# Layer 1's prompt attention: the two softmax maps summed on VectorE before PE transposes them

## The chip, the cores and the metric

The kernel runs on one NeuronCore of a Trainium2 chip. The metric is the device time of one execution in microseconds (us), from start to end of the program. The engines are called as the profile calls them: PE is TensorE (PEld its weight loads), DVE is VectorE, ACT is ScalarE, POOL is GpSimd, SP is the sync engine, which here only issues DMAs. PE's clock has two levels, 1.2 and 2.4 GHz; the profile gives the granted clock as a share of the higher one.

## What is computed

One inference step of a two-layer decoder: a prompt of 512 tokens and 8 sample sequences of one token each, with 2048 cached positions. Layer 0 is gated linear attention, layer 1 is differential attention over a shared key and value; each layer ends in a mixture of 16 experts. The part that matters here is layer 1's attention of the prompt, for 8 heads and 4 query blocks of 128 rows:

```
q1, q2 = q[..., :64], q[..., 64:]            # both maps have 64 columns of q and k
p1 = softmax(q1 @ k1.T + bias, axis=-1)      # bias: causal, ALiBi
p2 = softmax(q2 @ k2.T + bias, axis=-1)
o  = (p1 - lam * p2) @ v
```

In the same stage the sample sequences attend to their paged cache: for each sequence 16 pages of 128 keys and 128 values.

## The kernel before, in words

`stage_decoder` does both attentions. Each engine has its own program, in the order that is written out, and waits for the others by semaphores. A loop over slots `g` sets the order on every engine. In slots 0 to 31 four key pages are handled per slot: the pages arrive by DMA from SP, POOL multiplies three of them with the query (L1860) and DVE one (L2216), DVE sums all four (L2224, `sum_page`). PE multiplies the value pages of slot g-6 (`values`, L1925: 8 products, 16 entries in the trace). A softmax over each sample's scores has small steps on all engines, among them L2234, L2253 and L2259 on DVE, and one row of the output per sample (L1931, L1943, L2102, L2109).

The prompt's attention is cut into 32 units, u = 4h + i for head h and query block i; unit u covers n = i + 1 key blocks of 128. `Decoder.units(g)` puts two units into each of the slots 25 to 31 and three into each later one. For a unit:

- PE: `scores(u)` (L1981), two products into two PSUM banks.
- DVE: `block_scores(u)` (L2299) adds the bias, one instruction per map, into `SP[u % 2][0]` and `SP[u % 2][1]` in SBUF, and takes the negated row maximum of each (L2303).
- ACT: `powers(u)` (L2132), the two exponentials in place, each with its row sum into `ls`.
- DVE: `weigh(u)`: reciprocal of the second sum (L2280), then lm = -lam * l1 / l2 (L2282), which signals `c_ok`, then the reciprocal of the first sum (L2284).
- ACT: `second_weight(u)` (L2120) builds `dl`, the identity matrix times lm.
- PE: `finish(u)` forms the transposed weighted sum in PSUM: per block one product of the first map with the identity (L1991) and one of the second map with `dl` (L1992), accumulated. In f32 each such product is two entries in the trace.
- ACT: `c_copy(u)` (L2126) moves the result to SBUF; PE multiplies it with the values (L1997, the second half of `finish`); DVE scales and keeps it (`keep`, L2289).

The orders around it, written out by hand: DVE does weigh(u-1), keep(u-2), block_scores(u). ACT does second_weight(u-1), c_copy(u-1), powers(u). PE does scores(u), then, in the first unit of a slot, values, then sometimes the transposes of the next head's keys (L1968, `k_transpose`), then finish(u-1).

Of the kernel before, what the change touches and what calls it, by code (L numbers as in the profile page):

```python
# [9 lines left out]
ALU = mybir.AluOpType  # L10
ACT = mybir.ActivationFunctionType
# [1693 lines left out]
def stage_decoder(nc, ctx, m, a, dec):  # L1705
# [15 lines left out]
         "om_ok", "or_mm", "or_ev"))  # L1721
    k_tr, kt_ok, sc_mm, sb_ok, nb_ok, p_ok, c_ok, dl_ok, c_tr, c_cp, o_mm, o_ev = (sem(n) for n in
        ("k_tr", "kt_ok", "sc_mm", "sb_ok", "nb_ok", "p_ok", "c_ok", "dl_ok", "c_tr", "c_cp", "o_mm", "o_ev"))

# [22 lines left out]
    kth = [xtf[:, 512 * u:512 * (u + 1)] for u in range(2)]  # L1747
    dl = [xtf[:, 2 * 512 + u * P:2 * 512 + (u + 1) * P] for u in range(2)]
    xsq = m.xt[:, :, SEQ:SEQ + 32]
# [31 lines left out]
    with nc.Block() as block:  # L1781
# [81 lines left out]
        def _(pe):  # L1863
# [121 lines left out]
            def finish(u):  # L1985
                h, i = u // NQ, u % NQ
                pe.wait_ge(dl_ok, u + 1)
                wait(pe, c_cp, u)
                for j in range(i + 1):
                    block = slice(j * P, (j + 1) * P)  # L1990
                    nc.tensor.matmul(CT_B[:, block], SP[u % 2][0][:, block], m.ident[:, :], start=True, stop=False)  # L1991
                    last = nc.tensor.matmul(CT_B[:, block], SP[u % 2][1][:, block], dl[u % 2], start=False, stop=True)  # L1992
                last.then_inc(c_tr, 1)
# [67 lines left out]
        def _(s):  # L2061
# [55 lines left out]

            def second_weight(u):
                s.wait_ge(c_ok, u + 1)
                nc.scalar.activation(dl[u % 2], m.ident[:, :], ACT.Copy, scale=lm[u % 2]).then_inc(dl_ok, 1)  # L2120

            def c_copy(u):
# [28 lines left out]
            for g in range(1, dec.SLOTS + 4):  # L2151
# [23 lines left out]
                for u in dec.units(g):  # L2175
                    if u:
                        second_weight(u - 1)
                        c_copy(u - 1)
                    powers(u)
                    if u % NQ == 2 and u // NQ + 1 < HB:  # L2180
                        k_copy(u // NQ + 1)
                    if u == NQ * HB - 1:
                        second_weight(u)
                        c_copy(u)
# [8 lines left out]
        def _(v):  # L2193
# [84 lines left out]
            def weigh(u):  # L2278
                v.wait_ge(p_ok, u + 1)
                V.reciprocal(r1[u % NQ], ls[u % 2][:, 1:2])  # L2280
                v.drain()
                V.tensor_scalar(lm[u % 2], ls[u % 2][:, 0:1], r1[u % NQ], neg_lam, ALU.mult, ALU.mult).then_inc(c_ok, 1)  # L2282
                v.drain()
                V.reciprocal(r1[u % NQ], ls[u % 2][:, 0:1])  # L2284

# [154 lines left out]
```

## Time and profile before

| | us |
|---|---|
| median of 3 runs | 2092.64 |
| lowest and highest | 2091.74, 2094.64 |
| the profiled execution, its own time | 2090.62 |
| its span in the trace | 2088.8 |
| mean granted PE clock over the span | 0.863 |
| busy: PE, DVE, ACT, POOL | 1598.3, 751.6, 398.0, 365.3 |
| the 32 units of the prompt's attention | about 1288 to 1496 of the span |

The trace is of one execution. A busy time is the time with an instruction in the engine, whatever the engine does with it; an idle time is put down to the event that ended it.

### The profile page before, as it was taken

How to read it: one execution, taken by the hardware profiler on the slowest of the kernel's cores; microseconds unless marked ns; L12 is line 12 of the kernel's file. 1: busy time of each engine (PE TensorE's matmuls, PEld its weight loads, DVE VectorE, ACT ScalarE, POOL GpSimd, SP SyncE). 2: the span in 40 equal slices, each digit the busy share in tenths (PEclk: the TensorE clock that was granted, in tenths of full speed). 3: DMA queues.
4: the chain of work that ended last, by engine and by line, in shares of the span. 5: the costliest groups of instructions: out<-in, count | busy, mean ns of one | idle time of the engine just before them, and what ended most of it. 6: DMA issues, size and time to landing. Idle time of an engine off the chain costs nothing. (4 is left out here: it accounts for less than half of the span.)

```text
span 2088.8 us, 22132 instructions
## 1 busy us (share of the span) xinstructions
PE 1598.3 (77%) x7462; PEld 736.6 (35%) x7463; DVE 751.6 (36%) x1312; ACT 398.0 (19%) x763; POOL 365.3 (17%) x275
## 2 busy tenths in 40 slices
PE   5999976595379998846689888777585399989960
PEld 2333334142233333303236664444343233333320
DVE  1010144655400000064855566874365400000007
ACT  1010122011021122222011011334221012222212
POOL 0000000001000000032755556610001000000004
PEclk8999987597599999958789998899787599999985
DMA  8643522602599899799699999943121679999962
GB/s 331 261 179 116 209 81 62 234 11 83 222 406 428 337 389 429 313 359 344 242 395 362 400 392 406 357 175 122 60 76 53 242 282 374 410 428 427 429 266 100
DMA packets 122973, 563.55 MB, mean 270 GB/s; under 512 B 13613, under 2 KB 43054, under 8 KB 101371
## 3 DMA queue, kind: packets, MB, share of 16 engines
q1 hardware_dynamic: 98450, 496.63, 59.9%
q0 software_dynamic: 9088, 32.67, 4.3%
q10 hardware_dynamic: 15344, 33.08, 4.1%
q8 instruction: 51, 0.84, 0.2%
q14 instruction: 40, 0.33, 0.0%
HBM read 522.32 MB, written 40.03 MB: 269 GB/s over the span
## 5 line engine op out<-in xcount | busy, mean ns | idle before, releaser
L1488 PE MATMUL ps<-arena_w,arena_r 128*64 128x512 f32 x1664 | 379.7, 613 | 34.3 <-issue 29.4
L1488 PEld LDWEIGHTS ps<-arena_w,arena_r 128*64 128x64 f32 x1664 | 126.7, 142 | 281.1 <-issue 275.0
L1470 PE MATMUL ps<-arena_w,arena_r 128*64 128x512 f32 x832 | 190.2, 605 | 19.3 <-ACT arena_r L1518 19.3
L1565 DVE TENSOR_TENSOR arena_r<-arena_r,ps 128x512 f32<-128x512 f32 x38 | 26.2, 688 | 443.6 <-ACT arena_r L1535 443.6
L1860 POOL TENSOR_TENSOR arena_w<-arena_w,arena_r 128x1024 f32<-128x1024 f32 x48 | 115.8, 2419 | 101.4 <-DMA arena_w<-in_cache_k_dram 93.5
L1860 POOL TENSOR_TENSOR arena_r<-arena_r 128x1024 f32<-128x1024 f32 x48 | 115.7, 2414 | 51.4 <-DMA arena_r<-in_cache_k_dram 51.4
L1913 PE MATMUL ps<-arena_w,xt 128*128 128x256 f32 x512 | 123.7, 403 | 1.0 <-ACT xt L2073 1.0
L1091 POOL TENSOR_TENSOR x_res<-x_res,arena_m 128x1024 f32<-128x1024 f32 (+1 forms) x20 | 52.6, 2630 | 382.9 <-DVE x_res L1085 382.9
L512 PE MATMUL ps<-arena_w,xt 128*128 128x512 f32 x256 | 113.1, 598 | 0.4 <-PE ps L206 0.4
L1022 PE MATMUL ps<-arena_w,xt 128*128 128x512 f32 x256 | 111.1, 593 | 0.0
L1913 PEld LDWEIGHTS ps<-arena_w,xt 128*128 128x128 f32 x512 | 102.7, 203 | 18.5 <-issue 2.1
L1420 POOL COPY small<-idx 128x1 int32 (+1 forms) x38 | 6.9, 183 | 567.7 <-PE ps L1436 486.6
L1470 PEld LDWEIGHTS ps<-arena_w,arena_r 128*64 128x64 f32 x832 | 57.6, 138 | 125.7 <-issue 103.8
L1558 DVE COPY arena_r<-ps 128x512 f32<-128x512 f32 x38 | 26.3, 692 | 195.4 <-PE ps L1470 195.4
L1534 ACT ACTIVATE arena_r<-ps 64x512 f32<-64x512 f32 x38 | 22.4, 590 | 362.2 <-PE ps L1488 362.2
L2224 DVE TENSOR_REDUCE arena_r<-arena_w 128x16 f32<-128x1024 f32 x64 | 77.0, 1214 | 35.0 <-POOL arena_w L1860 34.9
L2224 DVE TENSOR_REDUCE arena_r<-arena_r 128x16 f32<-128x1024 f32 x64 | 76.6, 1210 | 20.8 <-POOL arena_r L1860 20.7
L1925 PE MATMUL ps<-arena_m,arena_r 128*16 128x512 f32 x512 | 70.5, 674 | 11.4 <-DMA arena_m<-in_cache_v_dram 11.4
L512 PEld LDWEIGHTS ps<-arena_w,xt 128*128 128x128 f32 x256 | 48.1, 191 | 66.4 <-issue 66.4
L1022 PEld LDWEIGHTS ps<-arena_w,xt 128*128 128x128 f32 x256 | 48.2, 190 | 60.0 <-issue 58.4
L1905 PE MATMUL ps<-xt,arena_w 128*128 128x512 f32 x128 | 63.5, 653 | 0.0
L471 PE MATMUL ps<-xt,arena_w 128*128 128x512 f32 x128 | 59.4, 619 | 4.1 <-PEq L248 3.7
(352 smaller groups left out, 1975.2 us busy)
## 6 DMA issues: line engine op xcount, KB each, us to landing
arena_w<-in_w_exp_gate_dram SPq DMA_DIRECT2D x38, 2048.0 KB, 11.8
arena_w<-in_w_exp_up_dram SPq DMA_DIRECT2D x38, 2048.0 KB, 18.6
arena_w<-in_w_exp_down_dram SPq DMA_DIRECT2D x38, 2048.0 KB, 18.6
arena_m<-in_cache_v_dram SPq DMA_DIRECT2D x128, 512.0 KB, 8.0
arena_w<-in_cache_k_dram SPq DMA_DIRECT2D x64, 512.0 KB, 9.4
arena_r<-in_cache_k_dram SPq DMA_DIRECT2D x64, 512.0 KB, 9.3
arena_w<-in_w_ada_dram SPq DMA_DIRECT2D x12, 2048.0 KB, 17.1
arena_m<-in_w_ada_dram SPq DMA_DIRECT2D x12, 2048.0 KB, 8.6
```

Source lines behind the costliest of these rows:

```text
L471: last = nc.tensor.matmul(m.ps[n % 2][:, :], w, m.xt[:, k, 0:SEQ], start=(k == 0), stop=(k == KT - 1))
L512: last = nc.tensor.matmul(m.ps[4 + n % 4][:, :], m.xt[:, k, i * P:(i + 1) * P], m.wr[c % 2][:, k, :], start=(k == 0), stop=(k == KT - 1))
L1022: last = nc.tensor.matmul(m.ps[(4 if n % 2 else 6) + c][0:r, :], m.xt[:, k, i * P:i * P + r], w[:, k, c * 512:(c + 1) * 512], start=(k == ...
L1091: nc.gpsimd.tensor_tensor(m.x[0:r, i, :], m.x[0:r, i, :], m.lnr[0:r, 1, :], ALU.add).then_inc(self.done, 1)
L1470: last = nc.tensor.matmul(psy[c][at:at + 64, :], ht[u][:, k, 64 * (1 - a):64 * (2 - a)], wd[u][:, k, c * 512:(c + 1) * 512], start=(k == 0 ...
L1488: last = nc.tensor.matmul(ps[at:at + 64, :], xgt[u][:, k, 64 * a:64 * (a + 1)], w[u][:, k, :], start=(k == 0), stop=(k == KT - 1), tile_po ...
L1558: V.tensor_copy(ys[u][:, 0:512], psy[0][:, :]).then_inc(y_v, 1)
L1860: G.tensor_tensor(kp[n % RING], kp[n % RING], qb[b % 2], ALU.mult).then_inc(pp_ok, 1)
L1905: last = nc.tensor.matmul(bank[:, :], w[:, k, part * P:(part + 1) * P], m.xt[:, k, 0:SEQ], start=(k == 0), stop=(k == KT - 1))
L1913: last = nc.tensor.matmul(bank[:, i * CW:(i + 1) * CW], m.xt[:, k, t], w[:, k, :], start=(k == 0), stop=(k == KT - 1))
L1925: last = nc.tensor.matmul(PSO[n][32 * g:32 * g + C, :], PR[b % 2][:, GRP * q + g, :], vp[GRP * (v % 2) + g][:, n * 512:(n + 1) * 512], sta ...
L2224: V.tensor_reduce(out=S[b % 2][:, j, :], in_=kp[n % RING].rearrange("p (c d) -> p c d", d=DHB), axis=AX.X, op=ALU.add).then_inc(ks_ok, 1)
```

## The change

Three engines are touched. DVE: `weigh(u)` gets one more instruction, `first = lm * second + first` over the unit's n x 128 columns, both maps read from SBUF and the result written over the first map; `c_ok` is signalled by it and no longer by the instruction that computes lm. ACT: `second_weight` goes, with `dl` and its semaphore. PE: `finish(u)` waits for `c_ok`, and its two accumulated products per block become one `transpose` of the first map.

```diff
             def finish(u):
                 h, i = u // NQ, u % NQ
-                pe.wait_ge(dl_ok, u + 1)
+                pe.wait_ge(c_ok, u + 1)
                 wait(pe, c_cp, u)
                 for j in range(i + 1):
                     block = slice(j * P, (j + 1) * P)
-                    nc.tensor.matmul(CT_B[:, block], SP[u % 2][0][:, block], m.ident[:, :], start=True, stop=False)
-                    last = nc.tensor.matmul(CT_B[:, block], SP[u % 2][1][:, block], dl[u % 2], start=False, stop=True)
+                    last = nc.tensor.transpose(CT_B[:, block], SP[u % 2][0][:, block], m.ident[:, :])
                 last.then_inc(c_tr, 1)
...
-            def second_weight(u):
-                s.wait_ge(c_ok, u + 1)
-                nc.scalar.activation(dl[u % 2], m.ident[:, :], ACT.Copy, scale=lm[u % 2]).then_inc(dl_ok, 1)
...
                     if u:
-                        second_weight(u - 1)
                         c_copy(u - 1)
                     powers(u)
...
                     if u == NQ * HB - 1:
-                        second_weight(u)
                         c_copy(u)
...
                 V.reciprocal(r1[u % NQ], ls[u % 2][:, 1:2])
                 v.drain()
-                V.tensor_scalar(lm[u % 2], ls[u % 2][:, 0:1], r1[u % NQ], neg_lam, ALU.mult, ALU.mult).then_inc(c_ok, 1)
+                V.tensor_scalar(lm[u % 2], ls[u % 2][:, 0:1], r1[u % NQ], neg_lam, ALU.mult, ALU.mult)
                 v.drain()
+                one, two = (SP[u % 2][j][:, 0:(u % NQ + 1) * P] for j in range(2))
+                V.scalar_tensor_tensor(out=one, in0=two, scalar=lm[u % 2], in1=one, op0=ALU.mult, op1=ALU.add).then_inc(c_ok, 1)
                 V.reciprocal(r1[u % NQ], ls[u % 2][:, 0:1])
```

## Rows read from the trace of the kernel before

**Rows 1.** Windows: busy us and entries of each engine, granted clock, DMA share, GB/s.
```profile
1285.00:1383.00 98.00, 72.30 (x429) 37.64 (x427) 83.97 (x153) 32.22 (x91) 50.80 (x22) 0.83 0.88 335
1383.00:1496.00 113.00, 86.24 (x515) 53.51 (x516) 54.20 (x165) 44.18 (x127) 0.00 (x0) 0.90 0.24 85
```

**Rows 2.** Waits of 1383 to 1496: engine, line, releaser, us in total, times, longest.
```profile
ACT arena_w L2126 <- PE ps L1992: 48.2, 20, 4.8
...
ACT arena_w L2132 <- DVE small L2303: 6.7, 10, 0.8
```

**Rows 3.** Groups by shape, 1284 to 1500: busy us, mean ns, idle before.
```profile
L1991 PE MATMUL ps<-ident,arena_w 128*128 128x128 f32 x160 | 36.6, 314 | 20.6 <-ACT xt L2120 20.6
...
L1992 PE MATMUL ps<-xt,arena_w 128*128 128x128 f32 x160 | 33.3, 293 | 0.0
...
L2299 DVE SCALAR_TENSOR_TENSOR arena_w<-arena_r,small,ps 128x512 f32<-128x512 f32 x16 | 11.2, 741 | 2.9 <-PE ps L1981 2.9
...
L1968 PE MATMUL ps<-ident,arena_w 128*128 128x128 f32 x32 | 5.9, 312 | 0.0
...
L2299 DVE SCALAR_TENSOR_TENSOR arena_w<-arena_r,small,ps 128x128 f32<-128x128 f32 x16 | 4.8, 339 | 1.8 <-PE ps L1981 1.8
```

**Rows 4.** Timeline around weigh(18), 3 blocks, and block_scores(19): start, us, engine, line.
```profile
1415.90 0.17 DVE L2280 RECIPROCAL small<-small 128x1 f32<-128x1 f32 x1 [1.37 <-ACT arena_w L2132]
...
1416.51 0.16 DVE L2284 RECIPROCAL small<-small 128x1 f32<-128x1 f32 x1
...
1416.84 1.40 DVE L2299 SCALAR_TENSOR_TENSOR arena_w<-arena_r,small,ps 128x512 f32<-128x512 f32 x2
...
1418.55 0.48 ACT L2126 COPY arena_w<-ps 128x384 f32<-128x384 f32 x1 [1.69 <-PE ps L1992]
...
1419.64 0.72 ACT L2132 ACTIVATE arena_w<-arena_w,small 128x512 f32<-128x512 f32 x1 [0.61 <-DVE small L2303]
...
1421.19 0.16 DVE L2280 RECIPROCAL small<-small 128x1 f32<-128x1 f32 x1 [0.79 <-ACT arena_w L2132]
```

**Rows 5.** Timeline around weigh(23) and finish(23), 4 blocks.
```profile
1448.57 0.17 DVE L2280 RECIPROCAL small<-small 128x1 f32<-128x1 f32 x1 [2.89 <-ACT arena_w L2132]
...
1449.12 0.40 ACT L2120 ACTIVATE xt<-ident,small 128x128 f32<-128x128 f32 x1 [0.58 <-DVE small L2282]
...
1449.57 0.49 PE L1991 MATMUL ps<-ident,arena_w 128*128 128x128 f32 x2 [1.04 <-ACT xt L2120]
...
1451.66 0.59 ACT L2126 COPY arena_w<-ps 128x512 f32<-128x512 f32 x1 [2.14 <-PE ps L1992]
1452.14 0.40 ACT L2132 ACTIVATE arena_w<-arena_w,small 128x128 f32<-128x128 f32 x1
```

**Rows 6.** Timeline: finish(27), 4 blocks, first product and the copy.
```profile
1467.87 0.79 PE L1991 MATMUL ps<-ident,arena_w 128*128 128x128 f32 x2 [1.76 <-ACT xt L2120]
...
1471.38 0.59 ACT L2126 COPY arena_w<-ps 128x512 f32<-128x512 f32 x1 [3.57 <-PE ps L1992]
```

**Rows 7.** Timeline: four transposes of a head's keys, at two places.
```profile
1312.34 1.12 PE L1968 MATMUL ps<-ident,arena_w 128*128 128x128 f32 x4
...
1389.87 0.66 PE L1968 MATMUL ps<-ident,arena_w 128*128 128x128 f32 x4
```

**Rows 8.** Timeline: the value products of one slot, at two places.
```profile
1308.79 3.62 PE L1925 MATMUL ps<-arena_m,arena_r 128*16 128x512 f32 x16 [2.33 <-DMA arena_m<-in_cache_v_dram]
...
1473.74 1.91 PE L1925 MATMUL ps<-arena_m,arena_r 128*16 128x512 f32 x16
```

**Rows 9.** By source: durations in ns, least/median/most; DVE instructions with two SBUF inputs.
```profile
L2216 DVE TENSOR_TENSOR arena_w<-arena_w,arena_r x16: 1217/1226/3410, 986.1 to 1353.8; 128x1024 f32<-128x1024 f32 x16
...
L1066 DVE SCALAR_TENSOR_TENSOR x_res<-x_res,arena_r x20: 1212/1226/1227, 435.3 to 2076.0; 128x1024 f32<-128x1024 f32 x16, 8x1024 f32<-8x1024 f32 x4
```

**Rows 10.** Timeline: POOL and DVE at 1352 to 1354.
```profile
1352.37 2.35 POOL L1860 TENSOR_TENSOR arena_w<-arena_w,arena_r 128x1024 f32<-128x1024 f32 x1 [0.21 <-DMA arena_w<-in_cache_k_dram]
...
1353.83 1.98 DVE L2216 TENSOR_TENSOR arena_w<-arena_w,arena_r 128x1024 f32<-128x1024 f32 x1
```

**Rows 11.** By source and timeline: the 32 weighs, and the last unit's copy.
```profile
L2280 DVE RECIPROCAL small<-small x32: 147/164/165, 1297.8 to 1489.3; 128x1 f32<-128x1 f32 x32
...
1493.10 0.59 ACT L2126 COPY arena_w<-ps 128x512 f32<-128x512 f32 x1 [2.88 <-PE ps L1992]
```

More of the change, by code:

```diff
@@ L1721, in stage_decoder @@
          "om_ok", "or_mm", "or_ev"))
-    k_tr, kt_ok, sc_mm, sb_ok, nb_ok, p_ok, c_ok, dl_ok, c_tr, c_cp, o_mm, o_ev = (sem(n) for n in
-        ("k_tr", "kt_ok", "sc_mm", "sb_ok", "nb_ok", "p_ok", "c_ok", "dl_ok", "c_tr", "c_cp", "o_mm", "o_ev"))
+    k_tr, kt_ok, sc_mm, sb_ok, nb_ok, p_ok, c_ok, c_tr, c_cp, o_mm, o_ev = (sem(n) for n in
+        ("k_tr", "kt_ok", "sc_mm", "sb_ok", "nb_ok", "p_ok", "c_ok", "c_tr", "c_cp", "o_mm", "o_ev"))
     kk, vv, qt = view(m.W, 8192, NQ, D), view(m.W, 12288, NQ, D), view(m.W, 16384, HB, SEQ)
@@ L1747, in stage_decoder @@
     kth = [xtf[:, 512 * u:512 * (u + 1)] for u in range(2)]
-    dl = [xtf[:, 2 * 512 + u * P:2 * 512 + (u + 1) * P] for u in range(2)]
     xsq = m.xt[:, :, SEQ:SEQ + 32]
```

## The prediction

> **What bounds the kernel now.** I read the windows first. The 32 units run from about 1288 to 1496, and the stretch splits in two. Up to 1383 the cache pages still run beside the units, and DVE is busy 83.97 of 98 us; behind that only value pages are left, and no engine is near full: PE 86.24, DVE 54.20, ACT 44.18 of 113 us [rows 1]. So the first part is mostly DVE's, the second a loop of waits. In the windows of 6 us DVE is at 5.1 to 5.8 from 1316 to 1386, so the little idle time before that lies ahead of 1316, where it waits for pages and for PE.
>
> The second view is the list of waits behind 1383, where the loop is to be seen. In program order ACT can't start the exponentials of unit u+1 before the copy of unit u, and can't start them before DVE has their maxima. The copy waited for PE 20 times, 48.2 us in all; the exponentials still waited for DVE's maxima after that in 10 units [rows 2]. Both ways begin at the same instruction, weigh(u)'s first reciprocal, and the later one sets the period. The timeline gives their lengths for every u:
>
> - DVE's way, where it ends last: after weigh(18) the bias additions start at +0.94, and the exponentials at +3.74, though the copy had been ready at +2.65 [rows 4]. For n = 1, 2, 3 blocks it is 2.66, 3.20, 3.74; for n = 4, with a one-block unit next, 2.14.
> - PE's way: after weigh(23) `dl` starts at +0.55, PE at +1.00, the copy at +3.09 and the exponentials at +3.57 [rows 5]. Its parts: 1.00 to PE, 0.30 + 0.446 n on PE (2.09 here), 0.16 to 0.48 of the copy.
>
> With every engine free, PE's way is the longer only for n = 4. It is also the longer where PE reaches `finish` late, behind the values or the rows of a sample.
>
> **The change part by part.** *PE.* Two products per block, four entries at about 0.11 us of pace, become one transpose. The key transposes show its price: one entry each (32 for 32), four in 0.66 us at the full clock and 1.12 at the half [rows 3, 7], so 0.27 + 0.13 (n-1); with 0.10 for a start from idle and 0.03 to the copy T(n) is 0.40, 0.53, 0.66, 0.79, and 1.22 for n = 4 at the half clock. *ACT.* `dl`, 0.40 us and 0.05 to PE, goes from the chain. *DVE.* One instruction with two SBUF inputs is added. No row has it at these widths. The nearest are L2299 with one input from PSUM, 0.339 at 128 columns and 0.741 at 512 [rows 3], slope 0.134 per block, and L1066 with both from SBUF, 1.226 at 1024 [rows 9], from which 0.16 + 0.133 n follows: 0.29, 0.42, 0.56, 0.69. It starts at +0.60, where the reciprocal now starts [rows 4], and what lies behind it moves by about 0.08 less than its duration, as between other DVE instructions here: e(n) = 0.22, 0.35, 0.48, 0.61. The upper bound is the whole duration.
>
> So DVE's way becomes 2.88, 3.55, 4.22, and 2.75 for n = 4; PE's way 1.50, 1.88, 2.25, 2.6. **DVE's way is now the longer everywhere but behind PE's queue.** Unit by unit from 1383 to the last copy at 1493 [rows 11]:
>
> - Eleven units whose maxima already ended last or together with the copy (n = 1: three, n = 2: four, n = 3: four) pay e(n), less what DVE already waits there for the scores: 0.3 + 1.4 + 1.9 = **+3.6**.
> - n = 4 at the full clock, unit 23: 3.57 to 2.75, **-0.8**.
> - n = 4 with the products at the half clock, units 15, 27, 31: PE takes 3.5 us for them where it took 2.09 [rows 5, 6]; 5.12, 5.01 to 3.04 in the first two, 1.5 in the last: **-5.5**.
> - Units behind values or rows keep PE's chain and gain only the shorter PE part: 16 and 28 0.35 each, 13 1.2 (the transposes of 12 and its own), 19 1.35, 22 1.05: **-4.3**.
>
> Sum behind 1383: -7.0.
>
> In the first part the ten weighs u = 2 to 11 add 4.4 us to a DVE that has no gap. Against it stand 0.86 from unit 1, whose finish DVE waited for until 1316, and 0.65 of DVE idle time at 1344: **+2.9**. Units 0 and 1 lie in the idle time before 1316 and cost nothing; without that cover they would cost 0.6.
>
> *The lock between DVE and POOL.* In the first part POOL multiplies keys 50.80 of 98 us [rows 1]. A DVE instruction with two SBUF inputs that meets a running POOL multiplication waits for its end: L2216 at 1353.83 took 1.98, and ended 1.23 after POOL's end at 1354.72 [rows 10]; its range is 1.217 to 3.410 [rows 9]. L2299, with one input from SBUF and one from PSUM, never took over 0.748. The new instruction is of the first kind. Placed at the old times, 8 of them (u = 2 to 9) meet 2.0 us of residue (units 2, 5, 7); placed at random, half of them meet 1.18 on average, 4.7. I take **+3.5**; bounds 0 and 9.4. DVE's other stalls of the kind (some 5.7 us in this part) may move either way.
>
> The Trainium skill says the same of the kind of instruction (SBUF — State Buffer, "Who interferes with whom"): two SBUF inputs contend with a POOL instruction that reads SBUF, and whoever comes second fully blocks. By that rule, the trace agrees; a sum without it would come out 3.5 lower.
>
> *The clock.* It is granted at 0.83 and 0.90 in the two parts [rows 1] and falls for a spell about once per head, after the units of 3 and 4 blocks, when PE waits longest for DVE. These pauses get longer and PE's work in them shrinks by about 0.31 us per block, 25 us over 80 blocks. The dense products of the 4-block unit, which now run through the end of a low spell, are gone, so that it reaches on to the values behind them. Values take 3.62 at the half clock and 1.91 at the full [rows 8]; with the scores and the PV products ahead of them up to 3.1 us for each of the four value chains that run mostly at the full clock. I take a quarter of 12.4: **+3**; bounds 0 and 12.
>
> Sum: 2.9 + 3.5 - 7.0 + 3 = +2.4. The profiled execution took 2090.62, its span 2088.8; 1.8 lies around it and doesn't change, nothing after the stage starts earlier than it, and its DMA queue is empty there (the stage's end moves the end one to one). That gives 2093.0 on the scale of this execution, and 2095.0 on that of the median, which is 2.0 above it.
>
> **The rivals.**
>
> *The relief wins (faster).* The new instructions fall between POOL's multiplications, as most do at the old times, and the clock stays: 2.9 - 7.0 = -4.1, 2088.5. For it: PE leads the list of waits. Against it: POOL is busy half the time. From a lock cost below about 3 with the clock unchanged it is a gain at all.
>
> *The gain on PE counts whole (faster).* 80 blocks x 0.31 and 32 x 0.45 are 39 us of PE and ACT work taken out; if PE bounded all units, 2054. Against it: DVE's way is at most 0.9 behind PE's even for n = 4 once the new instruction is in it. It would need the maxima never to end last, and they did 10 times of 20 [rows 2].
>
> *The clock falls further (slower).* Every value chain behind 1383 runs at the half clock: 9 us over my 3, 2104. For it: a third of PE's dense work goes. Against it: values and PV products, at 0.11 us an entry, stay. The Trainium skill has a rule for it (TensorE: Matmul & The Clock Gate, "Part 4: PE-mode transpose"): transposes don't count as busy work for the clock as matmuls do. By that rule even the remaining 10 us of transposes don't hold the clock up; the rows show transposes at either level and don't decide.
>
> *The lock at its worst (slower).* Each of the 8 waits 1.18: 9.4 in place of 3.5, 2101. It decides from about 6 on. A slower DVE lets POOL run further ahead, so where they meet isn't fixed.
>
> *The transpose costs as much as a product* (0.22 per block and not 0.13): only the units behind PE's queue see it, under 1 us. It changes nothing.
>
> **How the numbers follow.** A measurement of this kernel can tell about 0.2%, 4.2 us, from no change: below 2088.5 is faster, above 2096.8 slower. Gains and losses cancel as summed, between -4 and +5: 0.50, of it 0.39 within and 0.11 slower. Relief wins: 0.20, split 0.12 faster and 0.08 same, since it lies at the bound. Gain whole: 0.05. Clock 0.13, lock 0.12, both slower. So faster 0.17, same 0.47, slower 0.36. The likeliest is the sum, 2095. The range reaches from the relief (2088) to the lock at its worst (2101); outside lie the whole gain, part of the relief, and most of the clock's case, about 2 in 10.
>
> **What would show it.** L1992 and L2120 are gone and L1991's place has 80 entries. The new DVE instruction takes 0.29, 0.42, 0.56, 0.69 behind 1383, and some of those before 1370 over 1 us, all with POOL running. The exponentials wait for the maxima in nearly all units not behind values, at about 2.88, 3.55, 4.22, 2.75 after the reciprocal; the copy waits for PE far less than 48 us. The first part ends some 6 us later, the second is 4 us shorter. The granted clock behind 1383 is below 0.90. I am wrong if the first part grows by less than 3 or more than 10, if the second shrinks by more than 7 or not at all, or if the new instruction costs DVE more than its duration where POOL rests.

## The result and the profile after

| | before | after |
|---|---|---|
| median of 6 runs, us | 2093.64 | 2106.37 |
| lowest and highest | 2090.29, 2100.49 | 2102.19, 2110.50 |
| the profiled execution, its own time | 2090.62 | 2107.42 |
| its span | 2088.8 | 2105.6 |
| mean granted clock over the span | 0.863 | 0.841 |

The ratio is 1.0067, 95% interval 1.0046 to 1.0088: **the change makes the kernel slower by 0.67%** by that ratio; between the two medians lie 12.7 us, 0.61%. The forecast was 2095.0 with a range of 2088 to 2101, so it was wrong in size and its range too low. The share given to slower was 0.36, that to "within 0.2%" 0.47.

Windows of fixed time no longer hold the same work, since everything behind 1300 has moved. From here on I cut at two events of the kernel itself: the *first stretch* runs from weigh(0) to weigh(12), beside the cache pages, the *second* from weigh(12) to the copy of unit 31. For comparison the two fixed windows of [rows 1] come first. Windows of after (busy us and entries of PE, PEld, DVE, ACT, POOL; granted clock, DMA share, GB/s):

```profile
1285.00:1383.00 98.00, 61.85 (x292) 26.64 (x290) 87.64 (x139) 23.80 (x68) 51.78 (x23) 0.72 0.84 324
1383.00:1496.00 113.00, 82.38 (x385) 39.53 (x387) 68.03 (x190) 34.91 (x105) 0.00 (x0) 0.74 0.28 101
1299.55:1397.10 97.55, 62.35 (x296) 29.09 (x294) 90.38 (x155) 25.25 (x72) 43.58 (x18) 0.72 0.74 281
1397.10:1509.26 112.16, 81.12 (x355) 38.22 (x355) 63.40 (x184) 34.66 (x104) 0.00 (x0) 0.71 0.24 88
```

The same two stretches of before:

```profile
1297.77:1382.98 85.21, 64.35 (x385) 35.70 (x383) 74.67 (x143) 29.74 (x84) 43.29 (x18) 0.84 0.86 327
1382.98:1493.10 110.12, 83.97 (x505) 51.55 (x505) 54.07 (x164) 42.62 (x125) 0.00 (x0) 0.91 0.25 87
```

Two things are to be seen. In the first stretch DVE has 15.7 us more work (74.67 to 90.38) for 12 new instructions, whose bare durations would be 6.6 us; the stretch is 12.3 longer. In the second stretch PE has 150 entries fewer (505 to 355) and is busy hardly less (83.97 to 81.12), because its clock went from 0.91 to 0.71; that stretch is 2.0 longer where the forecast had it 4 shorter. Of the 16.8 us between the spans, 1.8 lie ahead of weigh(0), where the change does nothing yet, and 0.6 behind the second stretch.

**The new instruction, and the lock.** "Lock" is the prediction's word for what [rows 10] show: a DVE instruction with both inputs in SBUF that meets a running POOL multiplication goes on until that multiplication has ended. By source (ns: least, median, most) and by shape, after:

```profile
L2277 DVE SCALAR_TENSOR_TENSOR arena_w<-arena_w,small x32: 351/618/2595, 1300.1 to 1507.3; 128x128 f32<-128x128 f32 x8, 128x256 f32<-128x256 f32 x8, 128x384 f32<-128x384 f32 x8, 128x512 f32<-128x512 f32 x8
```

Undisturbed it takes 0.35, 0.48, 0.62 and 0.75 us for 1 to 4 blocks, 0.06 over my 0.29 to 0.69. Disturbed, it takes up to 2.6. The timeline of after at two places, with POOL's multiplication beside it:

```profile
1329.69 2.35 POOL L1859 TENSOR_TENSOR arena_w<-arena_w,arena_r 128x1024 f32<-128x1024 f32 x1 [0.18 <-DMA arena_w<-in_cache_k_dram]
1329.73 3.38 DVE L2208 TENSOR_TENSOR arena_w<-arena_w,arena_r 128x1024 f32<-128x1024 f32 x1
...
1375.63 2.36 POOL L1859 TENSOR_TENSOR arena_r<-arena_r 128x1024 f32<-128x1024 f32 x1 [0.50 <-DMA arena_r<-in_cache_k_dram]
1375.68 2.60 DVE L2277 SCALAR_TENSOR_TENSOR arena_w<-arena_w,small 128x256 f32<-128x256 f32 x1
```

At 1375.68 DVE starts 0.05 behind POOL and ends 0.29 behind POOL's end: a wait of 2.1 us for 0.48 of work. Six of the twelve were caught: units 1, 2, 3, 4, 6 and 9 took 2.27, 0.99, 2.09, 1.17, 2.51 and 2.60, which is 8.3 us over their bare durations. Of DVE's five page products in this stretch (L2208, L2216 before) two were caught as well, 3.4 us of excess where before had 0.75.

**DVE's way in the second stretch.** Timeline of after around weigh(18), 3 blocks, the place of [rows 4]:

```profile
1431.00 0.16 DVE L2272 RECIPROCAL small<-small 128x1 f32<-128x1 f32 x1 [1.37 <-ACT arena_w L2126]
...
1431.59 0.62 DVE L2277 SCALAR_TENSOR_TENSOR arena_w<-arena_w,small 128x384 f32<-128x384 f32 x1
...
1432.26 0.90 PE L1990 MATMUL ps<-ident,arena_w 128*128 128x128 f32 x3 [0.65 <-DVE arena_w L2277]
...
1432.44 1.40 DVE L2293 SCALAR_TENSOR_TENSOR arena_w<-arena_r,small,ps 128x512 f32<-128x512 f32 x2
...
1433.20 0.48 ACT L2120 COPY arena_w<-ps 128x384 f32<-128x384 f32 x1 [1.76 <-PE ps L1990]
...
1435.25 0.72 ACT L2126 ACTIVATE arena_w<-arena_w,small 128x512 f32<-128x512 f32 x1 [1.57 <-DVE small L2297]
```

The exponentials now start at +4.25 (1435.25 less 1431.00), where before had +3.74; 4.22 was forecast. The copy starts at +2.20, well before them, and no longer matters. Waits of after in the second stretch (us in total, times, longest):

```profile
ACT arena_w L2120 <- PE ps L1990: 55.1, 19, 7.1
...
ACT arena_w L2126 <- DVE small L2297: 14.9, 10, 1.9
```

Beside [rows 2], the wait for maxima doubled, 6.7 to 14.9, with the same 10 entries. The wait for PE did not shrink, 48.2 to 55.1, and its longest went from 4.8 to 7.1. Those are the units behind values. Timeline of PE behind unit 27, after, and then before:

```profile
1488.76 1.23 PE L1980 MATMUL ps<-xt,arena_w 64*128 64x256 f32 x4
1489.92 2.52 PE L1924 MATMUL ps<-arena_m,arena_r 128*16 128x512 f32 x16
...
1494.18 0.33 PE L1990 MATMUL ps<-ident,arena_w 128*128 128x128 f32 x1
```

```profile
1472.02 1.16 PE L1997 MATMUL ps<-arena_w 128*128 128x128 f32 x8 [0.68 <-ACT arena_w L2126]
1473.11 0.70 PE L1981 MATMUL ps<-xt,arena_w 64*128 64x256 f32 x4
```

The scores took 0.70 and now 1.23, the values 1.91 [rows 8] and now 2.52. The same products run at the lower level for part of their time. By shape over the whole stage (busy us, mean ns, idle before), after:

```profile
L1924 PE MATMUL ps<-arena_m,arena_r 128*16 128x512 f32 x224 | 37.7, 808 | 5.0 <-DMA arena_m<-in_cache_v_dram 5.0
...
L1995 PE MATMUL ps<-arena_w 128*128 128x128 f32 x160 | 36.4, 377 | 16.5 <-ACT arena_w L2120 16.5
...
L1990 PE MATMUL ps<-ident,arena_w 128*128 128x128 f32 x80 | 19.6, 354 | 40.2 <-DVE arena_w L2277 40.2
```

The same two groups of before:

```profile
L1925 PE MATMUL ps<-arena_m,arena_r 128*16 128x512 f32 x224 | 34.4, 744 | 7.0 <-DMA arena_m<-in_cache_v_dram 7.0
...
L1997 PE MATMUL ps<-arena_w 128*128 128x128 f32 x160 | 27.8, 307 | 16.5 <-ACT arena_w L2126 16.5
```

The 160 products with v went from 27.8 (307 ns each) to 36.4 us (377) with no change to their code, the values from 34.4 to 37.7. PE now waits 40.2 us for the new DVE instruction, where it waited 20.6 for `dl` [rows 3].

### The profile page after: what moved, and what is told of

It is laid out like the page before. It is cut to its first block and busy times, and to the rows that moved or that the text cites. A ratio compares the mean times of both kernels' runs of the same rounds, so it can differ in the third digit from the quotient of the medians.

```text
span 2105.6 us, 21652 instructions
## 1 busy us (share of the span) xinstructions
PE 1599.8 (76%) x7222; PEld 719.1 (34%) x7223; DVE 772.6 (37%) x1344; ACT 385.7 (18%) x731; POOL 366.0 (17%) x275
## 5 line engine op out<-in xcount | busy, mean ns | idle before, releaser
L2216 DVE TENSOR_REDUCE arena_r<-arena_w 128x16 f32<-128x1024 f32 x64 | 76.9, 1213 | 35.6 <-POOL arena_w L1859 35.5
L2216 DVE TENSOR_REDUCE arena_r<-arena_r 128x16 f32<-128x1024 f32 x64 | 76.7, 1211 | 21.5 <-POOL arena_r L1859 21.4
L1022 PEld LDWEIGHTS ps<-arena_w,xt 128*128 128x128 f32 x256 | 48.2, 190 | 60.0 <-issue 58.4
```

Source lines behind the costliest of these rows:

```text
L1022: last = nc.tensor.matmul(m.ps[(4 if n % 2 else 6) + c][0:r, :], m.xt[:, k, i * P:i * P + r], w[:, k, c * 512:(c + 1) * 512], start=(k == ...
L2216: V.tensor_reduce(out=S[b % 2][:, j, :], in_=kp[n % RING].rearrange("p (c d) -> p c d", d=DHB), axis=AX.X, op=ALU.add).then_inc(ks_ok, 1)
```

## The experiments

**Two theories.** *Mine behind the result* (theories L and C in the expectations, for its two halves, the lock and the clock): the loss has two parts that don't depend on each other. In the first stretch it is the exclusive access of two-SBUF-input instructions on DVE against POOL, about 10 us. In the second the clock falls because PE's dense work is gone, about 9 us, which eats a gain of 7. *The rival:* neither a lock nor the clock is at work. DVE is the bound, it got 0.35 to 0.75 us per unit more, and the rest is a shifted order of pages and units. A second rival for the second stretch: the gain of 7 was never there.

All stretches below are of one profiled execution each. For the second stretch the code of before was measured four times (before, early_new, add_sbuf, add_one: 110.1, 110.2, 116.5, 110.0), that of the first five times (before, late_new, warm_new, warm_more, late_four: 85.2, 81.6, 83.0, 86.4, 86.0). So a difference under 4 us between two single stretches says little, and the one second stretch of 116.5 shows that 6 us can come without any change of the code; what a single stretch shows has to be borne out by its units one by one.

**psum_in: the sum's second operand read from PSUM.** In the units' new instruction the first map is replaced by a bank of PSUM, so that only one input is from SBUF. It leaves the first map out of the sum, and with it layer 1's attention. Its values change which experts the tokens go to (36 tiles of experts are worked off in place of 38), so its total, 2071.03 and ratio 0.9918, can't be compared, nor with the 2099 that was expected; its stretches in the attention can.

```diff
-                V.scalar_tensor_tensor(out=one, in0=two, scalar=lm[u % 2], in1=one, op0=ALU.mult, op1=ALU.add).then_inc(c_ok, 1)
+                V.scalar_tensor_tensor(out=one, in0=two, scalar=lm[u % 2], in1=CT_B[:, 0:(u % NQ + 1) * P], op0=ALU.mult, op1=ALU.add).then_inc(c_ok, 1)
```

> As the changed kernel, but the new DVE instruction reads its second tensor from PSUM (the bank that holds the previous unit's sum), so that it has one SBUF input as the bias additions have; the first map is left out of the sum. One factor: the lock with POOL. Theory L (waits for POOL's multiplications carry the loss of the part with the key pages): none of the 32 instructions takes over 0.85 us where 6 took 0.99 to 2.60, the stretch from the first weigh to the thirteenth, 97.6 us in the changed kernel and 85.2 before, falls to 88 to 91, the time to about 2099. Rival C (PE's clock carries it: transposes and fewer products let it fall, and PE is late everywhere): the stretch stays above 95 and the time within 3 us of 2106.

By source and by windows of psum_in:

```profile
L2277 DVE SCALAR_TENSOR_TENSOR arena_w<-arena_w,small,ps x32: 346/546/749, 1295.3 to 1495.1; 128x128 f32<-128x128 f32 x8, 128x256 f32<-128x256 f32 x8, 128x384 f32<-128x384 f32 x8, 128x512 f32<-128x512 f32 x8
```

```profile
1294.77:1382.66 87.89, 62.97 (x296) 28.08 (x294) 79.73 (x154) 25.00 (x72) 43.17 (x18) 0.73 0.85 316
1382.66:1497.02 114.36, 79.54 (x355) 36.58 (x355) 63.28 (x184) 34.59 (x105) 0.00 (x0) 0.73 0.23 84
```

The same number of instructions of the same widths, none of them over 0.749 us, and the first stretch is 87.9 (88 to 91 had been expected) and not 97.6, at the same clock as after (0.73 and 0.72). So 9.7 us of the first stretch hang on the second SBUF input; the six waits above come to 8.3. DVE's five page products, which have two SBUF inputs in every kernel here, took 9.1 us in this run and 9.5 in after, so they are hardly part of the 9.7. That all five executions with the new instruction's two-input form in units 0 to 11 (after, early_new, two_products, one_product, add_sbuf) have a first stretch of 96.4 to 100.3, and none of the other eight is over 87.9, says that it isn't an accident of one execution. The 2.7 that are left over before hold the added durations, 2.2 us more of waiting in the page products (9.1 against 6.9), and what the fall of the clock from 0.84 to 0.73 costs; they aren't separated, and lie inside the spread of the old code. The second stretch stays at 114.4 with its clock at 0.73.

**add_sbuf and add_one: the lock on the kernel before.** To before's DVE program, behind `c_ok`'s signal, one instruction is added in units 0 to 11, whose result nobody reads. In add_sbuf it has the form of the change's; in add_one it is a sum over one map.

```diff
                 V.tensor_scalar(lm[u % 2], ls[u % 2][:, 0:1], r1[u % NQ], neg_lam, ALU.mult, ALU.mult).then_inc(c_ok, 1)
                 v.drain()
+                if u < 12:
+                    w = (u % NQ + 1) * P
+                    # add_sbuf:
+                    V.scalar_tensor_tensor(out=scrap[:, 0:w], in0=SP[u % 2][1][:, 0:w], scalar=lm[u % 2], in1=SP[u % 2][0][:, 0:w], op0=ALU.mult, op1=ALU.add)
+                    # add_one, in its place:
+                    V.tensor_reduce(out=scrap[:, 0:1], in_=SP[u % 2][1][:, 0:w], axis=AX.X, op=ALU.add)
```

> The kernel before, with one thing added in units 0 to 11: behind the signal of lm, DVE does the changed kernel's instruction (same widths, both inputs from SBUF) into a scrap tile that nobody reads. PE and ACT work as before. Theory L: the stretch from weigh 0 to weigh 12 grows from 85.2 (81.6 to 86.0 in four kernels that have it unchanged) to 93 to 99, as in the changed kernel (97.6), with several of the 12 added instructions over 1 us; the time is 2098 to 2104. Rival: the clock and PE's late finishes carry that stretch's loss; then only the 4.4 us of added durations come in, 86 to 91.

> The same place and widths, but the added instruction is a row sum of the second map into the scrap tile, with one SBUF input: about 0.07 us shorter each (0.28 to 0.69). Theory L: no added instruction takes over 0.75 us, and the stretch grows by the durations alone, 86 to 91 us; the time is 2092 to 2097. If this one too goes to 95, it is not the lock but any delay of DVE there.

Windows of the first stretch, and the new instruction by source; add_sbuf, then add_one:

```profile
1296.62:1396.96 100.34, 73.40 (x385) 41.22 (x383) 86.10 (x154) 29.80 (x84) 43.85 (x18) 0.76 0.74 281
```

```profile
L2287 DVE SCALAR_TENSOR_TENSOR xt<-arena_w,small x12: 352/684/2272, 1297.2 to 1390.9; 128x128 f32<-128x128 f32 x3, 128x256 f32<-128x256 f32 x3, 128x384 f32<-128x384 f32 x3, 128x512 f32<-128x512 f32 x3
```

```profile
1298.66:1384.62 85.96, 64.93 (x386) 35.28 (x384) 78.20 (x154) 29.72 (x84) 43.78 (x18) 0.86 0.84 323
```

```profile
L2287 DVE TENSOR_REDUCE xt<-arena_w x12: 286/487/687, 1299.3 to 1378.6; 128x1 f32<-128x128 f32 x3, 128x1 f32<-128x256 f32 x3, 128x1 f32<-128x384 f32 x3, 128x1 f32<-128x512 f32 x3
```

The bare durations differ by little (0.29 to 0.69 us for one form, 0.35 to 0.75 for the other). The first stretches differ by 14.3 us, 100.3 (93 to 99 had been expected) against 86.0 (86 to 91). Not all of that is the lock. DVE is busy 7.9 us longer (86.10 against 78.20): 4.3 in the four new instructions that were caught (units 1, 2, 3 and 4: 2.27, 0.97, 2.10, 1.18), 2.1 in a small sum of a sample's softmax (L2236, both inputs in SBUF, 2.51 us and not 0.42) that was caught too, 0.6 in the page products. Nearly all the rest is unit 7, whose period is 12.16 us in add_sbuf and 5.99 in add_one. Its window, and PE in it:

```profile
1355.65:1367.81 12.16, 11.48 (x39) 5.03 (x37) 5.88 (x13) 2.19 (x7) 3.44 (x2) 0.50 0.44 144
```

```profile
1355.54 3.61 PE L1926 MATMUL ps<-arena_m,arena_r 128*16 128x512 f32 x16
```

The clock was at its lower level through the whole of it, PE was busy 11.48 of 12.16 us with the values, a sample's rows and the unit's products, and DVE waited 6.0 us for the exponentials behind them. So the clock has its share in the first stretch as well once a low spell falls on the values. Whole: add_sbuf 2104.4, ratio 1.0068 (1.0041 to 1.0094), which is the loss of the whole change; add_one 2097.65, 1.0036 (1.0013 to 1.0059). Each lies a little above what was expected (2098 to 2104, 2092 to 2097). The medians are 6.8 us apart, and the intervals overlap. The traces show more than that, since add_sbuf's profiled execution (2109.53) is 5.1 above its median, and add_one's (2088.51) is the fastest of its ten, 9.1 below. So its trace has only 0.8 us of loss in the first stretch where its median has 6 in all, and where the rest lies isn't shown. The pair shows that the two-input form is caught and the other isn't; the size of the lock is psum_in's.

These four are also the first four of after (2.27, 0.99, 2.09, 1.17), so where the two engines meet there repeats itself from one kernel to the other. Why is only argued: the order of both is tied to the landing of the same pages. add_sbuf's second stretch, whose code is before's, took 116.5 at a clock of 0.84, where the other three have 110.0 to 110.2 at 0.91. Its units 16 and 28 took 8.17 and 8.32 in place of 5.86 and 6.66, nearly the 8.00 and 8.33 of after: the low spells fell on them. What moved the spells isn't shown; two facts lie near, that the first stretch had ended at another point of them, and that this execution took 5.1 us over its median.

**late_new and early_new: the change in one part of the units.** `new(u)` is `u >= 12` in late_new and `u < 12` in early_new; other units keep the old way, with `dl` and two products per block. DVE and ACT ask `new(u)` in the same way, which is left out below.

```diff
+    def new(u):
+        return u >= 12      # early_new: u < 12
+
+    def olds(n):
+        return sum(not new(u) for u in range(n))
...
-                pe.wait_ge(dl_ok, u + 1)
+                pe.wait_ge(c_ok, u + 1)
+                wait(pe, dl_ok, olds(u + 1))
...
+                    if new(u):
+                        last = nc.tensor.transpose(CT_B[:, block], SP[u % 2][0][:, block], m.ident[:, :])
+                        continue
```

> Units 0 to 11, beside the key pages, go the old way (dl on ACT, two products), units 12 to 31 the new way. Theory L: the loss lies in the part with the pages, so this is within 3 us of before, 2091 to 2097. Theory C: the clock is lost behind the pages as well, 2 to 5 us over before there, 2096 to 2100. By the prediction's own sum behind 1383 without a clock cost it would be 7 us faster than before.

> Units 0 to 11 go the new way, units 12 to 31 the old. Theory L: nearly the whole loss is here, 2103 to 2107. Theory C: half of it at most, 2097 to 2101. Together with the run that has the other half new, the two differences from before should add up to the 13 us of the whole change if the parts are independent.

Windows, late_new and then early_new:

```profile
1302.43:1384.02 81.59, 58.99 (x384) 34.47 (x383) 75.82 (x142) 29.72 (x84) 43.40 (x18) 0.90 0.88 330
1384.02:1495.75 111.73, 80.02 (x357) 38.53 (x355) 63.34 (x184) 34.68 (x105) 0.00 (x0) 0.71 0.25 86
```

```profile
1298.29:1395.48 97.19, 62.44 (x296) 28.97 (x294) 89.95 (x154) 25.21 (x72) 42.78 (x18) 0.71 0.75 284
1395.48:1505.69 110.21, 83.69 (x505) 51.56 (x505) 54.04 (x164) 42.60 (x125) 0.00 (x0) 0.91 0.26 91
```

late_new: 2092.36, ratio 1.0011 (0.9990 to 1.0031). early_new: 2103.81, 1.0083 (1.0058 to 1.0108). Both are as the two parts had it (2091 to 2097 and 2103 to 2107). The loss is that of the first 12 units; the other 20 come out even. In early_new the second stretch, which isn't changed, has its old length (110.2 against 110.1) and its old clock (0.91), though the first ran at 0.71; add_sbuf shows that this needn't be so. late_new's first stretch, not changed either, is 81.6 at 0.90, and before's was 85.2 at 0.84: within the spread of that code.

**two_products and one_product: PE's dense work back, DVE's sum kept.** Of the 80 blocks 50 lie in the second stretch. The transpose becomes products of the summed map with the identity. In two_products there are two per block, as many entries as before; in one_product one.

```diff
-                    last = nc.tensor.transpose(CT_B[:, block], SP[u % 2][0][:, block], m.ident[:, :])
+                    nc.tensor.matmul(CT_B[:, block], SP[u % 2][0][:, block], m.ident[:, :], start=True, stop=True)   # two_products alone
+                    last = nc.tensor.matmul(CT_B[:, block], SP[u % 2][0][:, block], m.ident[:, :], start=True, stop=True)
```

> As the changed kernel, but each block is turned by two products with the identity into the same place (both overwrite, the result is the same), so that PE has the entries it had before, while DVE keeps its new instruction and ACT stays relieved. Theory C: the granted clock between the first weigh and the last copy goes from about 0.73 back to 0.85 to 0.90, and though PE does more, the part behind the pages (112.2 us from weigh 12 to the last copy, 110.1 before) falls to 106 to 110; the time is 2098 to 2103. Theory L: the clock may rise, but the time stays at 2104 to 2108, or rises by the 80 times 0.32 us of PE work wherever PE is on the path, up to 2112.

> As the changed kernel, but each block is turned by one product with the identity and not by a transpose. If transposes keep the clock lower than products do, the granted clock behind weigh 12 rises from 0.73 to over 0.80 and the stretch of 112.2 us falls to 106 to 110. If only the missing work counts, clock and stretch stay: 0.73 to 0.77, 111 to 115, since a block takes 0.22 in place of 0.13 us. The stretch ahead of weigh 12 stays at 96 to 100 in both cases.

Windows of the second stretch, two_products and then one_product:

```profile
1399.28:1519.24 119.96, 89.75 (x505) 55.86 (x505) 62.98 (x184) 34.60 (x105) 0.00 (x0) 0.86 0.22 78
```

```profile
1397.87:1512.19 114.32, 79.94 (x405) 43.05 (x405) 63.14 (x184) 34.57 (x104) 0.00 (x0) 0.80 0.23 79
```

The clock of the stretch did as the theory has it: 0.71 with 50 transposes, 0.80 with 50 products, 0.86 with 100. The time did not. The clock theory had 106 to 110 for both, and measured were 120.0 and 114.3. one_product's length is in the range of the other reading (111 to 115), with a clock above the 0.77 of that reading; two_products' total is where theory L had it, 2104 to 2108 (whole: 2107.99, 1.0093, 1.0075 to 1.0111; and 2106.84, 1.0080, 1.0051 to 1.0110). The products now stand *behind* DVE's instruction and on the path: in units 15, 23 and 27 of two_products the exponentials start at +4.79, +5.50 and +5.37, where after had +3.03, +2.78 and +3.03 (before: +5.12, +3.57, +5.01). More PE work raises the clock, and where it lies on the path it costs more than the clock gives back. These two runs show that the clock rises with PE's work, not what it costs in time.

**warm_new and warm_more: PE work that lies in a wait.** On late_new, PE issues products of two identities whose result is overwritten, before it waits for `c_ok`, where it would be idle: four per unit in warm_new; in warm_more ten, and four in four-block units. Units behind values (13, 16, 19, 22, 25, 28) get none.

```diff
                 h, i = u // NQ, u % NQ
+                wait(pe, c_cp, u)
+                if u >= 12 and u not in (13, 16, 19, 22, 25, 28):
+                    for _ in range(4):        # warm_more: range(4 if u % NQ == 3 else 10)
+                        nc.tensor.matmul(CT_B[:, 0:P], m.ident[:, :], m.ident[:, :], start=True, stop=True)
                 pe.wait_ge(c_ok, u + 1)
                 wait(pe, dl_ok, olds(u + 1))
-                wait(pe, c_cp, u)
```

> The old way for units 0 to 11, the new way behind, and in the units behind that do not follow values PE issues four products of the identity with itself into the bank that the transposes overwrite, while it waits for DVE: filler work, nothing of the result depends on it. Theory C (behind the pages the fallen clock takes back what the shorter PE way gives, 9 us of it): the granted clock from weigh 12 to the last copy goes from 0.75 to 0.88 or more, and the 111.7 us of that stretch fall to 102 to 106; the time is 2083 to 2088, faster than before. Rival F: the filler delays the scores and finishes behind it as much as the clock gives, 109 to 113 us, 2090 to 2094.

> As the run with four filler products, but ten in the units of 1 to 3 blocks, where PE waits about 2 us for DVE. With four the clock went only to 0.83 and the stretch to 109.7 us. Theory C: with ten the clock goes to 0.92 or more and the stretch to 102 to 106. Rival F, that filler holds up what is behind it: 110 to 116.

Windows of the second stretch, warm_new and then warm_more, and the timeline of warm_more behind unit 27, with the fillers of unit 29:

```profile
1378.17:1487.83 109.66, 86.53 (x469) 48.98 (x467) 63.15 (x184) 34.70 (x104) 0.00 (x0) 0.83 0.25 88
```

```profile
1382.99:1488.04 105.05, 88.40 (x589) 57.86 (x587) 63.14 (x184) 34.59 (x105) 0.00 (x0) 0.95 0.27 93
```

```profile
1466.48 0.70 PE L1987 MATMUL ps<-xt,arena_w 64*128 64x256 f32 x4
1467.11 1.91 PE L1931 MATMUL ps<-arena_m,arena_r 128*16 128x512 f32 x16
...
1470.77 0.33 PE L2002 MATMUL ps<-ident,arena_w 128*128 128x128 f32 x1
...
1473.75 4.54 PE L1996 MATMUL ps<-ident 128*128 128x128 f32 x20
```

Four idle products lift the clock only to 0.83, and the stretch to 109.7: I had asked for at least 0.88 and 102 to 106, a miss, halfway in both. Ten lift it to 0.95, and the stretch falls from 111.7 to 105.1 (0.92 or more and 102 to 106 were expected). Scores and values are back at 0.70 and 1.91.

These are single stretches, so the units have to bear it out. From late_new to warm_more, units 16, 19, 22 and 28, which stand behind values and have no filler of their own, went from 7.81, 8.86, 9.36 and 8.32 us to 5.48, 7.86, 7.09 and 6.06, and unit 15 from 6.19 to 4.60: 9.4 us gained. Where a filler lies in the way it costs. Unit 29 went from 5.07 to 7.73, because its ten fell into a low spell and took 4.54 us (2.4 to 2.5 at the full clock), and unit 20 from 4.04 to 4.90. This is the run that prices the clock: nothing but work in PE's waits was added, units without it became shorter, and the change's second stretch is 6.6 us shorter on balance, 5.1 below before's. How much of the summed gain of 7.0 (which gives 103.1) is there at the full clock is shown only so far: 5.1, with the fillers' cost in it. Whole: warm_new 2090.0, 1.0007 (0.9988 to 1.0026); warm_more 2085.94, 0.9988 (0.9965 to 1.0012), against late_new's 1.0011. 2083 to 2088 had been expected of warm_new. The order of the totals fits, but the intervals overlap, so the price rests on the traces.

**late_four: the change where it had paid.** By [rows 5] and [rows 6] only four-block units had PE's way as the longer one. `new(u)` is `u >= 12 and u % NQ == 3`; the diff is late_new's but for that line.

> The new way only for the 4-block units 15, 19, 23, 27, 31, the others as before. By the prediction's ledger these five carry 2.1 + 1.35 + 0.8 + 2.0 + 1.5 us of gain without the +3.6 of the others, and most of PE's work between them stays: the stretch from weigh 12 to the last copy falls from 110.1 to 102 to 105, the time to 2083 to 2088. If the clock is what decides, it falls behind these units on to the values: 107 to 111, 2088 to 2093.

Windows of its second stretch:

```profile
1386.10:1494.11 108.01, 81.06 (x447) 45.56 (x445) 57.72 (x169) 40.62 (x120) 0.00 (x0) 0.86 0.26 90
```

2086.69, ratio 0.9974 (0.9954 to 0.9995); one execution took 2907.55 at a mean clock of 0.565, where the others had 0.856 to 0.864. It isn't in the ratio, and I have no explanation for it. The ledger's gains alone had the stretch at 102 to 105; it came to 108.0, in the range of the rival (107 to 111), that the clock falls behind these units: it is 0.86 where before had 0.91, and units 16, 25 and 28, which aren't changed, went from 5.86, 4.54 and 6.66 to 7.75, 7.09 and 8.88. The 2.1 us that are left of the gain are less than two single stretches can tell apart. The whole is faster, by 0.05 to 0.46% by its interval, and within the 2083 to 2088 of the gains.

**first_ahead: the shorter way for PE without DVE's sum.** Back to the kernel before. The products of the first map need neither `dl` nor lm, only the exponentials. So they are issued ahead of the wait for `dl`, and the second map's are accumulated behind it. `start` now stands on the unit's first product alone and `stop` on its last, since the blocks' sums are open in the bank together. Nothing is added to DVE and no work leaves PE.

```diff
             def finish(u):
                 h, i = u // NQ, u % NQ
-                pe.wait_ge(dl_ok, u + 1)
+                pe.wait_ge(p_ok, u + 1)
                 wait(pe, c_cp, u)
                 for j in range(i + 1):
                     block = slice(j * P, (j + 1) * P)
-                    nc.tensor.matmul(CT_B[:, block], SP[u % 2][0][:, block], m.ident[:, :], start=True, stop=False)
-                    last = nc.tensor.matmul(CT_B[:, block], SP[u % 2][1][:, block], dl[u % 2], start=False, stop=True)
+                    nc.tensor.matmul(CT_B[:, block], SP[u % 2][0][:, block], m.ident[:, :], start=(j == 0), stop=False)
+                pe.wait_ge(dl_ok, u + 1)
+                for j in range(i + 1):
+                    block = slice(j * P, (j + 1) * P)
+                    last = nc.tensor.matmul(CT_B[:, block], SP[u % 2][1][:, block], dl[u % 2], start=False, stop=(j == i))
```

> The kernel before, with one change: finish(u) issues the products of the first map as soon as the exponentials are done, and waits for dl only ahead of the products of the second map; DVE and ACT are untouched. PE's way gets shorter by up to 0.22 us per block, and PE's work stays and lies earlier, so the clock should hold. If the loop behind the pages is bound as the prediction has it, the units of 4 blocks gain 0.8 at the full clock and 1.5 to 2 at the half, those behind values little: 110.1 falls to 103 to 107, the time to 2084 to 2089. If PE's waits for scores and values bind instead, nothing: 109 to 111, 2089 to 2093.

Windows of its two stretches, and its timeline around weigh(23), the place of [rows 5]:

```profile
1300.36:1384.15 83.79, 66.66 (x388) 36.00 (x386) 74.94 (x143) 29.74 (x84) 43.19 (x18) 0.84 0.86 331
1384.15:1485.92 101.77, 80.00 (x503) 48.90 (x503) 54.05 (x164) 42.71 (x125) 0.00 (x0) 0.96 0.27 94
```

```profile
1445.54 0.16 DVE L2283 RECIPROCAL small<-small 128x1 f32<-128x1 f32 x1 [2.51 <-ACT arena_w L2135]
1445.55 1.16 PE L1991 MATMUL ps<-ident,arena_w 128*128 128x128 f32 x8
...
1446.09 0.40 ACT L2123 ACTIVATE xt<-ident,small 128x128 f32<-128x128 f32 x1 [0.58 <-DVE small L2285]
...
1446.55 1.15 PE L1995 MATMUL ps<-xt,arena_w 128*128 128x128 f32 x8
1447.73 0.59 ACT L2129 COPY arena_w<-ps 128x512 f32<-128x512 f32 x1 [1.25 <-PE ps L1995]
1448.22 0.40 ACT L2135 ACTIVATE arena_w<-arena_w,small 128x128 f32<-128x128 f32 x1
```

While DVE computes lm and ACT builds `dl`, PE does the first half of its work. The exponentials start at +2.68, where before had +3.57. Unit 15 went from 7.15 to 4.71, 27 from 5.91 to 3.59, 23 from 4.48 to 3.59; the units of DVE's way and those behind values stayed within 0.04, but for 13 (6.30 to 4.55). **2079.31, ratio 0.9953 (0.9933 to 0.9972): it beats both kernels.** The clock is 0.96, the highest of all; that the same work has fewer pauses in it would explain that, but isn't shown apart. The stretch of 101.8 is below the 103 to 107 and the total below the 2084 to 2089 that I had put down. So part of what the change was to bring, PE's way in the four-block units, was to be had by an order alone.

## Why the prediction was wrong, by its own steps

- **What bounds the two parts**: right in the main. The first stretch grew when DVE got work, though add_sbuf's unit 7 shows PE's clock setting the pace there too; in the second DVE's way is the longer nearly everywhere but behind the values. It came out at 2.91, 3.58, 4.25 and 2.78 for n = 1, 2, 3 and 4, where 2.88, 3.55, 4.22 and 2.75 stood.
- **The new instruction's duration**: 0.06 too low in each width. As DVE's way shows, that moved 0.03.
- **Durations in the first part, +2.9**: not refuted, and not shown. psum_in has +2.7 and add_one, with a somewhat shorter instruction, +0.8; both lie inside the spread of the old code's first stretch, and 2.2 us of psum_in's are other waits.
- **The lock, +3.5: this is the first term that failed.** It costs 9.7 (97.6 less 87.9), just over the upper bound of 9.4 that was kept as a rival. The error was to place the new instructions at the old times: there units 2, 5 and 7 met 2.0 us of residue; in the trace of after units 1, 2, 3, 4, 6 and 9 met 8.3. (A small misreading had no part in it: in [rows 10] DVE ended 1.09 after POOL's end, not 1.23, and the waits of after end likewise a little less than a bare duration after it.) The page products met 2.6 more than before, but in psum_in they met nearly as much. The old times can't be used, because every wait moves the next start, and both engines hang on the same pages. By the rule of the Trainium skill (SBUF — State Buffer, "Who interferes with whom": a DVE instruction with two SBUF inputs contends with a POOL instruction that reads SBUF, one with at most one SBUF input does not outside DVE's two-port modes, and a reduction on this chip never does), the trace agrees: up to 2.60 us for two inputs from SBUF, never over 0.749 with one from PSUM, never over 0.687 for the reduction.
- **The ledger of the second part, -7.0**: right in kind, its size shown only in part. Unit 27 went from 5.92 to 3.94 (its period from weigh to weigh), 23 from 4.48 to 3.70, unit 31's copy from 3.84 to 2.55, 13 from 6.30 to 4.96. The eleven units of DVE's way pay 5.1 together where +3.6 stood: most 0.25 to 0.53, unit 20 0.08, and 24 and 25, around which the clock was low for a spell, 0.80 and 0.64. warm_more, near the full clock, is at 105.1, 5.1 below before, with its fillers in it.
- **The clock, +3: the second term that failed.** The stretch is 2.0 longer and not 4 shorter. 6.6 us of that come back in warm_more; if the ledger's -7.0 holds whole, the clock took 9. That is three times the +3, and the rival "the clock falls further" in kind, at less than its price (9 over the 3, so 12). It is where it was expected: unit 16 went from 5.86 to 8.00 and 28 from 6.65 to 8.33 for a forecast gain of 0.35 each; 19 and 22 gained 0.34 and 0.20 in place of 1.35 and 1.05; 15 gained 0.96 and not 2.1, because its products with v took 2.08 us and not 1.16. These five alone are 7.5 us off the forecast. Taking a quarter of the upper bound had no row behind it. late_new, warm_new and warm_more (0.71, 0.83, 0.95 for 111.7, 109.7, 105.1 us), and in warm_more the units behind values, show both that the clock is the cause and that PE's idle work buys it back; how much of what lies beyond 6.6 is the clock's stays open.
- **The chances.** The two slower rivals had 0.13 and 0.12, as if apart. Both mechanisms worked at once: the lock cost 6 over its term and the clock up to 6 over its own, and 2095 and 6 each is 2107, against 2106.4. That it comes out so closely is in part luck, since the terms were taken from single executions. Neither needed an accident: half of DVE's new instructions under a busy POOL, and a third of PE's dense work taken out of a loop whose clock already fell about once per head, were both in the rows.

The rival that there is neither lock nor clock falls by psum_in, by the durations in add_sbuf against add_one, and by warm_more. That there was no gain falls by warm_more, which is 5.1 below before. The first twelve units alone cost 0.83% (early_new); the other twenty alone 0.11% (late_new), whose interval holds 0. Together 0.94%, a little over the whole's 0.67%, with overlapping intervals.

## What to carry to other kernels

A DVE instruction with two SBUF inputs beside a working POOL has a range that reaches from its own duration to that of POOL's whole multiplication: here 12 of them, of 0.35 to 0.75 us, cost 9.7 us beyond their durations. How often they meet can't be read from the old times of the trace, since every wait moves the next start. Work taken from PE ahead of a wait is not a gain by its duration: count which products behind it will run at the lower clock, and look first for an order that lets PE do the part whose inputs are ready while the others still compute the rest. Where two costs are uncertain and both have a mechanism that the rows already show at work, put their upper halves together into the range.

## What was not expected of the hardware

- **Transposes and the clock.** With the same 50 blocks the second stretch was granted 0.71 for transposes and 0.80 for products, and 0.86 for 100 products. The Trainium skill (TensorE: Matmul & The Clock Gate, "Part 4: PE-mode transpose") says that a transpose doesn't count as PE's busy work in the same way. The runs go the same way and don't decide it, since an f32 product is also two entries where a transpose is one.
- **Little idle work is enough.** Ten products of two identities per unit in PE's idle time, four in the four-block ones, raised the clock from 0.71 to 0.95, and the stretch took 105.1 and not 111.7 us.
- **The clock in the first stretch.** The five executions of the old code go with it: 81.6 at 0.90, 83.0 at 0.88, and 86.4, 86.0 and 85.2 at 0.84. But psum_in, with more work on DVE, took only 87.9 at 0.73. What the clock costs where DVE is the bound isn't shown apart.
- **Unexplained**: what moved the low spells in add_sbuf's second stretch (116.5 with the code of before), and late_four's single execution of 2907.55.
